# Three reorderings in a two-block transformer kernel: lambda and latents ahead of modulation pieces on VectorE, the odd layer's modulation sums one projection group later, and the experts' gate/up weights in whole transfers

## The reference

```python
mod = cond @ ada_w[i] + ada_b[i]            # six vectors of 1024: sh1, sc1, g1, sh2, sc2, g2
h = rms_norm(x, norm_g[i, 0]) * (1.0 + sc1) + sh1
x = x + g1 * mixer(h)
h = rms_norm(x, norm_g[i, 1]) * (1.0 + sc2) + sh2
x = x + g2 * ffn(h)                         # experts, or PEER
# experts: (silu(x_blk @ w_gate[e]) * (x_blk @ w_up[e])) @ w_down[e]
# even mixer: ckv = rmsnorm(ckv, kv_norm); an index score picks 64 keys of each query
#             lam = exp(sum(lv[0] * lv[1])) - exp(sum(lv[2] * lv[3])) + lam_init
# odd mixer:  attention with a forget gate, q, k, v, f = split(h @ w_in)
```

## Time and profile before

| | |
|---|---|
| median of 3 runs | 2399.66 us (2399.15 to 2404.76) |
| the profiled execution, its own time | 2395.93 us |
| span of its profile | 2394.2 us |
| busy in the span: PE, DVE, POOL, ACT | 80%, 56%, 23%, 14% |
| moved by DMA | 894.79 MB, mean 374 GB/s |
| the stages by the trace (us) | first mixer to about 190, experts to 660, even mixer to 833, PEER to 1536, odd mixer to 1685, PEER to the end |

### The profile page before, as it was taken

How to read it: one execution, slowest core, us unless ns; L and a number is a source line. 1 busy time by engine, 2 the same in 40 slices (tenths; PEclk the granted TensorE clock), 3 DMA queues, 4 the chain that set the end, 5 groups by cost and what they waited for, 6 DMA issues and landing times.

```text
span 2394.2 us, 24630 instructions
## 1 busy us (share of the span) xinstructions
PE 1903.9 (80%) x9143; PEld 1018.9 (43%) x9143; DVE 1350.3 (56%) x3261; ACT 326.2 (14%) x812; POOL 554.3 (23%) x567
## 2 busy tenths in 40 slices
PE   6998666667678699988877777788999988777776
PEld 4665333333366464444322222374644444233222
DVE  2633100000058658767877776555487788778865
ACT  1052000000021420010100000203311110000000
POOL 1000000000000114434434343100134444344332
PEclk9999988887889799999999999999999999999999
DMA  9987999999988269999999999893399999999997
GB/s 389 410 247 318 427 427 427 426 428 426 400 316 340 96 234 405 422 421 421 410 422 421 421 406 421 347 366 131 146 409 421 422 421 416 421 420 411 418 422 298
DMA packets 151224, 894.79 MB, mean 374 GB/s; under 512 B 18908, under 2 KB 31036, under 8 KB 64060
## 3 DMA queue, kind: packets, MB, share of 16 engines
q0 software_dynamic: 73728, 536.90, 54.2%
q1 hardware_dynamic: 77372, 356.25, 37.5%
HBM read 889.68 MB, written 3.42 MB: 373 GB/s over the span
## 4 chain that ended last, share of the span: by engine, by line
DMA 48%; PE 31%; DVE 12%; issue 4%; ACT 3%; SPq 1%; POOL 0%; DVEq 0%; POOLq 0%; PEldq 0%; ACTq 0%
DMA sb_area<-in_peer_uv,sb_peer_e 29%; DMA sb_area<-in_moe_w_gu 14%; PE psum L1653 13%; DMA sb_area<-in_ada_w 4%; PE psum L1155 3%; PE psum L1128 3%; PE psum L1121 2%; DVE sb_area L2253 2%; DVE sb_area L2271 2%; PE psum L1349 1%; DVE sb_area L1803 1%; PE psum L1374 1%; PE psum L1609 1%; DVE sb_area L2139 1%; PE psum L1333 1%
## 5 line engine op out<-in xcount | busy, mean ns | idle before, releaser
L1653 PE MATMUL psum<-sb_area 128*128 128x512 f32 x2048 | 978.4, 615 | 237.2 <-DVE sb_area L2253 233.6
L2271 DVE CUSTOM_DVE_ANT_0 sb_area<-sb_area 128x1024 f32<-128x1024 f32 x512 | 625.9, 1224 | 269.4 <-DMA sb_area<-in_peer_uv,sb_peer_e 266.9
L751 POOL DMA_INDIRECT sb_area<-in_peer_uv,sb_peer_e x512 | 536.7, 1048 | 1036.3 <-PE psum L1653 730.0
L1653 PEld LDWEIGHTS psum<-sb_area 128*128 128x128 f32 x2048 | 374.8, 193 | 720.8 <-DVE sb_area L2253 377.2
L1349 PE MATMUL psum<-sb_area 128*32 128x256 f32 x2048 | 168.7, 488 | 129.8 <-DMA sb_area<-in_moe_w_gu 126.5
L1888 DVE COPY sb_area<-psum 128x128 f32<-128x128 f32 x32 | 9.3, 292 | 392.2 <-PE psum L1361 392.2
L1066 ACT ACTIVATE sb_small<-sb_small 128x2 f32<-128x2 f32 x256 | 52.1, 204 | 1150.6 <-DVE sb_small L2271 1150.6
L2253 DVE SCALAR_TENSOR_TENSOR sb_area<-sb_ident,sb_small,sb_area 128x128 f32<-128x128 f32 x512 | 156.6, 347 | 56.6 <-ACT sb_small L1066 52.0
L1121 PE MATMUL psum<-sb_area 128*128 128x256 f32 x784 | 177.3, 389 | 3.2 <-DVE sb_area L1725 3.2
L733 POOL TENSOR_SCALAR_AFFINE_SELECT sb_area<-sb_area 128x256 f32<-128x256 f32 x1 | 0.4, 407 | 749.3 <-DVE sb_area L2081 749.3
L1803 DVE SCALAR_TENSOR_TENSOR sb_area<-sb_area,sb_c_silu 128x2048 f32<-128x2048 f32 x56 | 131.6, 2351 | 72.9 <-DMA sb_area<-in_ada_w 70.1
(11 more groups left out here) (299 smaller groups left out, 1388.3 us busy)
## 6 DMA issues: line engine op xcount, KB each, us to landing
sb_area<-in_moe_w_gu SPq DMA_DIRECT2D x64, 2048.0 KB, 32.9
sb_area<-in_ada_w SPq DMA_DIRECT2D x72, 1024.0 KB, 12.1
sb_area<-in_moe_w_dn SPq DMA_DIRECT2D x32, 2048.0 KB, 26.6
sb_area<-in_peer_w_q SPq DMA_DIRECT2D x8, 2048.0 KB, 8.1
sb_area<-in_sb_w_in SPq DMA_DIRECT2D x6, 2048.0 KB, 21.0
sb_area<-in_odd_w_in SPq DMA_DIRECT2D x6, 2048.0 KB, 10.9
sb_area<-in_even_w_in SPq DMA_DIRECT2D x5, 2048.0 KB, 12.4
sb_area<-in_peer_uv,sb_peer_e POOLq DMA_INDIRECT x512, 13.0
```

What stands on the lines that cost most here:

```text
L751: pool.indirect_dma_start(uv_rows[s], None, rows, bass.IndirectOffsetOnAxis(ap=peer_e[:, m:m + 1], axis=0)).then_inc(named(f"uv_loaded{s}" ...
L1653: last = pe.matmul(ps[:, 4 + 2 * t + half, :], diag[:, s, :], uv_rows[s][:, D + half * HALF:D + (half + 1) * HALF], start=(k == 0), stop=( ...
L2271: dve.tensor_tensor_reduce(uv_rows[s][:, 0:D], uv_rows[s][:, 0:D], h_tok[:, m // P, :], 1.0, 0.0, ALU.mult, ALU.add, dots[:, m % BODY:m % ...
```

## The change

It has three parts, and a fourth that only renames (the values of the semaphore `latent_dve` get names, in the new order).

1. Even layer, DVE: lambda's products and sums stand ahead of all pieces; the latents' variance and scaling stand after 3 pieces, not 4. `copy_row(4)` stands after head 1, not head 3.
2. Odd layer, PE: the sums of thirds 7 and 8 stand after groups 3 and 5, not 2 and 4, their turns after groups 4 and 6, not 3 and 5.
3. Experts: gate/up weights come in one 4 MB transfer, except for the experts 3 and 31, which keep two halves. For the others SP waits for `gu_done` alone and PE has no wait at the middle.

```diff
+        HALVED = (EXPERT_BUFS, EXPERTS - 1)
...
                 for e in range(EXPERT_BUFS, EXPERTS):
-                    sp.wait_ge(named("gu_half"), p * EXPERTS + e - EXPERT_BUFS + 1)
-                    load_gu(e, (0,))
-                    sp.wait_ge(named("gu_done"), p * EXPERTS + e - EXPERT_BUFS + 1)
-                    load_gu(e, (1,))
+                    if e in HALVED:
+                        sp.wait_ge(named("gu_half"), p * EXPERTS + e - EXPERT_BUFS + 1)
+                        load_half(e, 0, named(f"gu_loaded{e % EXPERT_BUFS}"))
+                        sp.wait_ge(named("gu_done"), p * EXPERTS + e - EXPERT_BUFS + 1)
+                        load_half(e, 1, named(f"gu_rest{e}"))
+                    else:
+                        sp.wait_ge(named("gu_done"), p * EXPERTS + e - EXPERT_BUFS + 1)
+                        load_gu(e)
...
-            pe.wait_ge(named("latent_dve"), 5)
+            pe.wait_ge(named("latent_dve"), CKV_TURNED)
...
             for i, (n, g) in enumerate(odd[:-2]):
                 project(n, g)
-                if i in (2, 4):
-                    sum_third(6 + i // 2)
                 if i in (3, 5):
-                    turn_row(6 + i // 2)
+                    sum_third(7 + i // 5)
+                if i in (4, 6):
+                    turn_row(7 + i // 6)
...
             at = BY_STAGE["even"][0]
-            ada_pieces(at, at + 4)
+            dve.wait_ge(named("even_vec_loaded"), 16 * 3)
+            lam_pairs = lam_vec.rearrange("p (a b) d -> p a b d", b=2)
+            step(dve.tensor_tensor(lam_prod[:, :, :], lam_pairs[:, :, 0, :], lam_pairs[:, :, 1, :], ALU.mult))
+            dve.tensor_reduce(lam_sum, lam_prod[:, :, :], AX_X, ALU.add).then_inc(named("latent_dve"), 1)
+            dve.tensor_scalar(subln_col, subln_raw, 1.0 - LAM_INIT, None, ALU.mult).then_inc(named("latent_dve"), 1)
+            ada_pieces(at, at + 3)
             dve.wait_ge(named("latent_act"), 2)
...
-            ada_pieces(at + 4, at + 11)
-            dve.wait_ge(named("even_vec_loaded"), 16 * 3)
...
+            ada_pieces(at + 3, at + 11)
             dve.wait_ge(named("latent_act"), 4)
...
-                if h in (3, 7):
+                if h in (1, 7):
                     copy_row(4 + h // 7)
```

More of the change, by code:

```diff
@@ L398, in two_block_kernel @@
         assert SM + 6 * THIRD <= AREA - REL_HEADS * MAPW - 4 * HEAD - 3
+        LAM_SUM, SUBLN, KV_VAR, KV_SCALED, CKV_TURNED = range(1, 6)
         LAM_INIT = 0.8 - 0.6 * math.exp(0.0)
@@ L595, in _, with load_gu, load_half @@
                              ).then_inc(named("rel_stored"), 16)
[L596 to L601, removed]
+            def load_gu(e):
+                sp.dma_start(moe_gu[e % EXPERT_BUFS].rearrange("p k q f -> p (k q f)"), I["moe_w_gu"][e]
+                             ).then_inc(named(f"gu_loaded{e % EXPERT_BUFS}"), 16)
+            def load_half(e, half, loaded):
+                cols = slice(half * HALF_GU, (half + 1) * HALF_GU)
+                sp.dma_start(moe_gu[e % EXPERT_BUFS].rearrange("p k q f -> p (k q f)")[:, cols], I["moe_w_gu"][e][:, cols]
+                             ).then_inc(loaded, 16)
             def load_down(e):
@@ L961, in softmax_attention @@
                                        ACT.Square).then_inc(named("diff_act"), 1)
-                        act.wait_ge(named("latent_dve"), 4)
+                        act.wait_ge(named("latent_dve"), SUBLN)
                         act.activation(oT[:, 4:8, :].rearrange("p h t -> p (h t)"), ps[:, 2:4, :].rearrange("p b n -> p (b n)"),
@@ L977, in _ @@
                                accum_out=kv_ssq[:, t:t + 1]).then_inc(named("latent_act"), 1)
-            act.wait_ge(named("latent_dve"), 1)
+            act.wait_ge(named("latent_dve"), KV_VAR)
             act.activation(kv_std, kv_std, ACT.Sqrt).then_inc(named("latent_act"), 1)
@@ L981, in _ @@
             take(*even[2])
-            act.wait_ge(named("latent_dve"), 3)
+            act.wait_ge(named("latent_dve"), LAM_SUM)
             act.activation(lam_exp, lam_sum, ACT.Exp).then_inc(named("latent_act"), 1)
@@ L989, in idx_relus @@
                 act.activation(idx_relu[h % 2], ps[:, 4 + h % 2, 0:MAPW], ACT.Relu, scale=HEAD ** -0.5).then_inc(named("idx_relu_done"), 1)
-            act.wait_ge(named("latent_dve"), 2)
+            act.wait_ge(named("latent_dve"), KV_SCALED)
             for i in range(4):
@@ L1345, in gate_up @@
                     for k in range(KC):
-                        if k == KC // 2:
-                            pe.wait_ge(named(f"gu_loaded1_{e % EXPERT_BUFS}"), loaded)
+                        if k == KC // 2 and e in HALVED:
+                            pe.wait_ge(named(f"gu_rest{e}"), p * 16 + 16)
                         for q in range(QUAD):
@@ L1510, in _ @@
             project(*even[2])
-            pe.wait_ge(named("latent_dve"), 2)
+            pe.wait_ge(named("latent_dve"), KV_SCALED)
             for c in range(LATENT // P):
@@ L2056, in _ @@
             last.then_inc(named("latent_dve"), 1)
-            ada_pieces(at + 4, at + 11)
-            dve.wait_ge(named("even_vec_loaded"), 16 * 3)
-            lam_pairs = lam_vec.rearrange("p (a b) d -> p a b d", b=2)
-            step(dve.tensor_tensor(lam_prod[:, :, :], lam_pairs[:, :, 0, :], lam_pairs[:, :, 1, :], ALU.mult))
-            dve.tensor_reduce(lam_sum, lam_prod[:, :, :], AX_X, ALU.add).then_inc(named("latent_dve"), 1)
-            dve.tensor_scalar(subln_col, subln_raw, 1.0 - LAM_INIT, None, ALU.mult).then_inc(named("latent_dve"), 1)
+            ada_pieces(at + 3, at + 11)
             dve.wait_ge(named("latent_act"), 4)
```

3 lines of the change are left out of this document (1 added, 2 removed).

## The result

The changed kernel takes **2389.26 us** (median of 5 runs, 2384.87 to 2390.99) against 2399.66 of before: ratio 0.9943, 95% interval 0.9919 to 0.9967, so 7.9 to 19.4 us less. The two medians lie 10.4 us apart, the ratio means 13.7; both are inside that interval. The forecast was 2387.3, with 2380 to 2395.5 as the whole range.

The account below looks back on a forecast made before the run. Transfers were taken to set the experts and the even mixer, PE's list the odd mixer's end. Terms -10.3, -0.5 and -1.6 sum to -12.4 us, from 2399.66 to 2387.3, with a range of 2380 to 2395.5.

Parts of the forecast that it names:

- The odd layer, -10.3: Odd mixer: moving PE's sums and turns brings the first scores earlier, -10.3 us, from -11 to -8.5.
- the bound of -11: Odd mixer: the largest gain allowed for the term of -10.3 us, whose other end was -8.5.
- the restart behind the new wait: Odd mixer, PE after its 2.6 us wait for group 5's weights: 0 to 1.4 us lost to the clock, 0.3 taken.
- The even layer, -0.5: Even mixer: PE's 6.17 us wait becomes one of 7.5 elsewhere; term -0.5 us, bounds -3 and +2.
- The lower bound of -3: Even mixer: -3 us if the shifted wait lets PE enter the attention at full clock.
- The experts, -1.6: Experts: whole gate/up transfers with longer rows raise the DMA rate; term -1.6 us, ends 0 and 3.
- the next doubling gives half of that, 0.7%: Experts' gate/up rows: doubling once gave 1.4%; if overhead is per row, the next gives 0.7%, 1.9 us.
- The sum, -12.4: Whole kernel: -10.3 - 0.5 - 1.6 = -12.4 us, from 2399.66 to 2387.3, or to 2383.5 from the profiled execution.
- Partly given back: Odd layer: group 5's weights land later, starting it 4.8 us later; odd term -4, time 2393.7; chance 0.15.
- Experts become slower: Experts: if the transfer queue runs dry, each of 27 adds 1.9 us, 51 in all; time 2438; chance 0.03.
- Fixed cost for each transfer: Experts: 30 fewer transfers save at most 4 us, time 2383; chance 0.06 together with a warmer even layer.

Follow-up runs that it names:

- first sum only: Kernel before with only the sum of third 7 moved behind group 3, the sum of third 8 left behind group 4: ratio 1.0008.
- even alone: Kernel before with only the even mixer's lambda, latent and row 4 edits: ratio 0.9995.
- experts alone: Kernel before with only the gate/up weights of 30 experts sent in whole transfers of 32 KB rows: ratio 0.9990.
- quarters: Kernel before with each half of an expert's gate/up weights sent as two 1 MB transfers with 8 KB rows: ratio 1.0020.
- all whole: The whole change with the fourth and last expert's gate/up weights sent whole as well: ratio 0.9949.

## Why the prediction was right, step by step

**The odd layer, -10.3.** Profile -11.03, timed alone -9.8. The steps held one by one (measured times in brackets; this profile's stage starts 1.1 us later): first sum at 1591.3 (1591.92), the turn of row 7 at 1606.3 (1606.84), group 5 at 1609.4 behind 2.6 us of wait (1609.91, 2.48), group 6 without one, first scores at 1639.5 (1639.95). That -11.03 lies just past the bound of -11 comes from group 5: it started 68.1 us behind the stage's start, where the forecast has 68.7. That PE's list sets this stage's end was the reading on which all rested; "first sum only" confirms it from the other side. One bound was short: I priced the restart behind the new wait at 0 to 1.4 us from two waits in the experts. It cost 0 in the profile of after and in two more, 1.5 and 3.0 in two others.

**The even layer, -0.5.** Profile -0.53; timed -1.2, within its error of nothing. The wait went where it was forecast (7.5 us; 8.08). The lower bound of -3 assumed that entering the attention at full clock is worth something. It happened, 0.49 us for the first scores where before had 0.80, and gave nothing: from the first scores to the output products it is 46.91 us, before 46.96.

**The experts, -1.6.** The rate came out as 429, inside 427 to 431, and timed alone it is -2.4. In the one pair of profiles the stage was 0.73 us longer. That is scatter: the last combine lies at 656.83 to 660.72 in the four profiles with halves (mean 658.5) and at 655.91 to 658.66 in the seven with whole transfers (657.3), 1.2 us apart with ranges that overlap. The working, "the next doubling gives half of that, 0.7%", had its first step from one window of 5 us in another stage. It now stands on the experts' own numbers: two thirds of the bytes in that window are gate/up, so 423, 427 and 429 GB/s mean 1.4% and 0.7% on them, with rates rounded to 1 GB/s, and by the packets' 313, 613 and 1215 ns it is 2.1% and 0.9%.

By the Trainium skill ("DMA: Bandwidth & Descriptors", "Why small descriptors are slow") the same two steps would be 0.6% and 0.3%, an estimate from its three cycles. The runs agree with the halving and show two to three and a half times the size.

**The sum, -12.4, and its base.** The three parts alone multiply to 0.9959 x 0.9995 x 0.9990 = 0.9944, the whole is 0.9943: no sign that an edit helps or hinders another, though the interval of the whole (0.9919 to 0.9967) would hide some 6 us. The medians differ by 10.4 us. The sum against the profiled execution, 2383.5, missed its successor by 5.8 us, and the choice of the median as the base was what kept the forecast near. Part of that is luck: the profile of before had its attention, output and search in 96.65 us, while first sum only, even alone, experts alone and quarters needed 100.3 to 101.5. A forecast of -12.4 between 10.4 by the medians and 13.7 by the ratio is closer than these runs can tell.

**The rivals.** "Partly given back" is not what the change does: weights 4.8 us later did not come, group 5 started 68.1 to 68.6 us behind the stage's start in the five profiles that keep this wait, forecast 68.7. Its cold clock did come: in all whole the odd layer took 101.5 us in place of 98.1. "Experts become slower" needed the queue to run dry; the share stayed at 1.00. "Fixed cost for each transfer" would have shown in quarters.

The Trainium skill's 2.0 us for each transfer (same page, "Anatomy of one DMA", which gives it for transfers that GpSimd issues, while SP issues these) would make 128 us of quarters' 64 extra transfers if nothing hid it, an estimate by the page. The run shows 4.8, so with the queue full nearly all of such a cost, if it is there, is hidden.

## What to carry to other kernels

A wait for another engine's result is gone only when the waiting engine has other work for all of it; ask what is late next, then move both consumers, not one. Where transfers fill a stage, neither a removed wait nor half the vector work on the arriving pieces shortened it; what did was the rate, and there doubling the rows was worth 0.5% to 1%. Judge a difference of a few us by a stage's length over several profiles: one profile of before was 4 us fast in stages that nobody had touched.

## What was not expected of the hardware

Two transfers of 64 partitions each, with 32 KB rows, in place of one of 128: the experts' rate fell from 429 to 234 GB/s, landing took 61.2 us in place of 33.3, and the DMA engines still showed as busy (1.01). Each packet took longer: a row of 32 KB 2529 ns (median) in place of 1215, and a row of 16 KB, most of them of the down weights, which still went to 128 partitions in one transfer, 900 in place of 613. The Trainium skill ("DMA: Bandwidth & Descriptors", "Rules for kernel authors") says that transfers to two halves of the partitions gain nothing, as both use the same engines; here they lost nearly half of the rate. Why is not shown.

The same kind of wait, 2.5 to 3.5 us ahead of group 5, cost its own length in three profiles (2.48, 2.70, 2.96) and 1.5 and 3.0 us more in two (3.15, 3.45), by the clock that PE was granted behind it. Whether the wait's length decides this, five profiles do not show.
